# The big scratch tensor of a two-network float32 kernel, laid out in another order in SBUF

## What is computed

```python
def first_block(h):                      # per layer i of 2
    h = h + 0.5 * swiglu(rmsnorm(h, ffn1_norm[i]), gate, up, down)     # 1024 -> 2816 -> 1024
    u = rmsnorm(h, mix_norm[i]) @ w_in[i]
    y = concat([y_mla, y_mlstm, y_fnet])                               # the mixers, from u
    h = h + y @ w_out[i]
    h = h + 0.5 * swiglu(rmsnorm(h, ffn2_norm[i]), gate, up, down)
    e = rmsnorm(p[i] @ ple_w_proj[i], ple_post_norm[i])
    h = h + sigmoid(rmsnorm(h, ple_gate_norm[i]) @ ple_w_gate[i]) * e

def second_block(x):                     # per layer l of 2
    mod = cond @ ada_w[l] + ada_b[l]                                   # shift, scale, gate
    h = rmsnorm_2(x, norm_mix[l]) * (1 + sc_m) + sh_m
    x = x + gt_m * hybrid_mixer(h, ...)      # window attention, HGRN2, gated delta rule, w_out
    h = rmsnorm_2(x, norm_ffn[l]) * (1 + sc_f) + sh_f
    x = x + gt_f * swiglu_2(h, gate, up, down)
```

## Time and profile before

| | us |
|---|---|
| median of three timed executions (lowest, highest) | 3909.55 (3904.68, 3914.15) |
| the profiled execution: its time | 3909.84 |
| its span, first to last instruction | 3908.1 |
| TensorE busy (share of the span) | 3732.5 (96%) |
| VectorE busy | 2213.7 (57%) |
| ScalarE busy | 1296.8 (33%) |
| GpSimd busy | 730.3 (19%) |

### The profile page before, as it was taken

One profiled execution on the slowest core, in us unless ns is written; L12 is line 12 of the kernel. 1 busy time (PEld: TensorE's weight loads), 2 busy tenths in 40 slices (PEclk: granted clock), 3 DMA queues, 4 the chain that ended last, 5 costly groups with the idle time before them and its releaser, 6 DMA issues. The chain is left out here.

```text
span 3908.1 us, 42134 instructions
## 1 busy us (share of the span) xinstructions
PE 3732.5 (96%) x16630; PEld 2876.4 (74%) x16630; DVE 2213.7 (57%) x2994; ACT 1296.8 (33%) x1873; POOL 730.3 (19%) x434
## 2 busy tenths in 40 slices
PE   8999998999999999998999989888999999989999
PEld 6888733888878888635888866686888766867887
DVE  6554557655564455457655576665544557755443
ACT  3222235522242223335422343444222343443221
POOL 3432002343213430001444013020000020200000
PEclk9999998999999999998999999798999998989999
DMA  4443201444323442102444322001233220012232
GB/s 169 140 135 107 94 13 33 134 138 129 121 93 126 134 132 93 60 23 81 138 131 137 97 78 62 4 1 65 87 95 100 81 77 21 1 49 82 95 99 81
DMA packets 92947, 345.43 MB, mean 88 GB/s; under 512 B 10832, under 2 KB 11088, under 8 KB 91856
## 3 DMA queue, kind: packets, MB, share of 16 engines
q1 hardware_dynamic: 92752, 342.74, 27.1%
HBM read 340.60 MB, written 2.10 MB: 88 GB/s over the span
## 5 line engine op out<-in xcount | busy, mean ns | idle before, releaser
L383 ACT ACTIVATE w_hi<-raw 128x1024 fp32r<-128x1024 f32 (+2 forms) x540 | 559.5, 1038 | 1927.9 <-PE ps L327 1912.6
L325 PE MATMUL ps<-xs_hi,w_hi 128*128 128x512 f32 x2472 | 982.1, 397 | 35.6 <-DVE xs_lo L544 16.5
L326 PE MATMUL ps<-xs_lo,w_hi 128*128 128x512 f32 x2472 | 970.5, 393 | 0.0
L327 PE MATMUL ps<-xs_hi,w_lo 128*128 128x512 f32 x2472 | 970.1, 392 | 0.0
L393 DVE TENSOR_TENSOR w_lo<-raw,w_hi 128x1024 fp32r<-128x1024 f32 (+2 forms) x540 | 673.9, 1249 | 125.9 <-ACT w_hi L383 125.7
L325 PEld LDWEIGHTS ps<-xs_hi,w_hi 128*128 128x128 f32 x2472 | 468.8, 190 | 161.1 <-issue 33.7
L326 PEld LDWEIGHTS ps<-xs_lo,w_hi 128*128 128x128 f32 x2472 | 469.9, 190 | 99.0 <-issue 3.6
L327 PEld LDWEIGHTS ps<-xs_hi,w_lo 128*128 128x128 f32 x2472 | 469.2, 190 | 98.9
L325 PE MATMUL ps<-hd_hi,w_hi 128*128 128x512 f32 x1320 | 527.0, 399 | 4.7 <-DVE hd_lo L486 3.5
L327 PE MATMUL ps<-hd_hi,w_lo 128*128 128x512 f32 x1320 | 523.8, 397 | 0.0
L326 PE MATMUL ps<-hd_lo,w_hi 128*128 128x512 f32 x1320 | 523.8, 397 | 0.0
(11 more groups left out here) (454 smaller groups left out, 4341.1 us busy)
## 6 DMA issues: line engine op xcount, KB each, us to landing
raw<-in_ffn_gu SPq DMA_DIRECT2D x264, 512.0 KB, 3.8
arena<-in_ada SPq DMA_DIRECT2D x64, 768.0 KB, 5.6
raw<-in_ffn_dn SPq DMA_DIRECT2D x96, 448.0 KB, 3.4
raw<-in_in_t SPq DMA_DIRECT2D x60, 512.0 KB, 3.7
raw<-in_ffn_dn SPq DMA_DIRECT2D x48, 512.0 KB, 3.5
raw<-in_out SPq DMA_DIRECT2D x32, 512.0 KB, 3.7
raw<-in_pleg SPq DMA_DIRECT2D x16, 512.0 KB, 3.6
raw<-in_in_r SPq DMA_DIRECT2D x8, 512.0 KB, 3.8
```

The costliest lines, as they stand in the source:

```text
L325: T.matmul(bank, lhs_hi(k), rhs_hi(k), start=(first and k == 0), stop=False)
L326: T.matmul(bank, lhs_hi(k), rhs_lo(k), start=False, stop=False)
L327: mm = T.matmul(bank, lhs_lo(k), rhs_hi(k), start=False, stop=(last and k == kt - 1))
L383: A.activation(self.hi[:, n % HL, 0:size], raw[:, n % RAW, 0:size], ACT.Copy).then_inc(self.high_done, 1)
```

## The change

Only numbers change: where the parts of the arena lie. Not one instruction is added, removed or moved on any engine, nor is any wait.

```diff
     SPLIT = 2 * DT * S
-    REST = 13088
-    SPARE = 1808
-    LINE = 128
-    HD_AT, REST_AT = 0, SPLIT
-    X_AT = SPLIT + REST
+    REST = 13064
+    SPARE = 1920
+    LINE = 32
+    HD_AT, X_AT = 0, SPLIT
     HL_AT = X_AT + SPLIT
     SPARE_AT = HL_AT + 2 * HL * CW
-    WORDS = SPARE_AT + SPARE
+    REST_AT = SPARE_AT + SPARE
+    WORDS = REST_AT + REST
     fence_at = -(-nc.sbuf_base // LINE) * LINE
...
     def work_space():

-        return Space(HD_AT + DT * S, SPLIT - DT * S), Space(X_AT, WORDS - X_AT)
+        return Space(HD_AT + DT * S, SPLIT - DT * S), Space(X_AT, REST_AT - X_AT)
```

## The result

The changed kernel takes 3877.19 us (median of four, 3871.53 to 3878.38) against 3909.28 us for the kernel before in the same comparison: a ratio of 0.9917, 95% interval 0.9904 to 0.9929, so 32.1 us less. The profiled execution took 3878.38 us around a span of 3876.6. Forecast were 3879.8 us and a gain of 30.0.

A forecast was written before the change was run, and what follows sets the result against it. TensorE's pace was taken to bound the kernel; 25.2 + 4.3 + 0.5 = 30.0 us off 3909.8 gave 3879.8 us (80%), own range 3872 to 3890, range for all 3870 to 3900.

The forecast's parts named there:

- The bound: Whole kernel: TensorE's own pace sets the time, weight preparation is ahead, and the gain reaches the end undiminished.
- `hd`: 25.2 us: 3960 matmuls streaming hd, put at distance 0, speed up to the pace of xs: 25.2 us gained.
- `ys`: 4.3 us: 768 matmuls streaming ys, put at distance 0, each gain 5.6 ns: 4.3 us.
- The swapped product: 0.5 us: 96 matmuls with hd as weights go from 232.3 to 226.8 ns: 0.5 us gained.
- `xs` and alignment: nothing: xs and w by w keep distance 0 by 512; starts 32 bytes past a multiple of 128 cost nothing.
- the rival of 3960 us: All split matmuls: the shorter pace needs starts at multiples of 64 or 128 bytes, so 50 us slower; 7% chance.
- Regions: 3948 us: Split matmuls: an operand below byte 131072 costs pace; 42.8 us lost on hd and xs, ys gains 4.3; 5% chance.
- Mixers and other engines: 0 with 2 us each way: Mixers' moved buffers and other engines' operations: no change, with 2 us each way allowed for the mixers' small operations.
- A multiple of 512 bytes: Split matmuls: about 226.8 ns where stream and weights lie such a distance apart, 232.3 to 233.3 ns elsewhere.

The follow-up runs named there:

- `old_order`: Kernel before with REST 13120 words in place of 13088, putting xs and the ring 128 bytes further; 3876.63 us against 3909.37, ratio 0.9918.
- `order_alone`: Changed kernel with a 128-byte gap that restores the old remainders by 512 between stream and weights; 3907.18 us against 3906.23 for the kernel before, ratio 1.0004.
- `w_lo_off`: Changed kernel with only w_lo moved, by 128 bytes; 3924.81 us against 3906.23 for the kernel before, ratio 1.0058.
- `all_off`: Changed kernel with the weight ring moved by 128 bytes, so xs, hd and ys are at remainder 384; 3938.36 us against the kernel before's 3906.23.

## Why the prediction was right

*The bound.* It took TensorE's pace as what sets the time, and a shorter pace as fully paid out. TensorE's busy time fell by 30.9 us and the span by 31.5; no wait took the place.

*`hd`: 25.2 us.* The stretches over `hd` are 25.7 us shorter, here and in `old_order`.

*`ys`: 4.3 us.* Its mean interval at full clock went from 232.6 to 227.0 ns, which gives 4.3 us. In the lengths of the stretches the granted clock hid it in the first pair of traces (-0.1 us) and added to it in `old_order` (-5.7), so no single trace shows the term by its stretches.

*The swapped product: 0.5 us.* Measured 0.5.

*`xs` and alignment: nothing.* Right: every split operand now starts 32 bytes past a multiple of 64, and 226.7 ns is the same pace. This also removes the rival of 3960 us. It was the step with the thinnest ground, and that ground was misread, so here the forecast was lucky. The prediction took the 68 matmuls of line 317 as a row in which some read an operand 32 bytes past a multiple of 64 and some don't. By the offsets (`uq` and `ukv` start at words 7688 and 9992 of the mixers' part, the other operand of each product on a multiple of 256 bytes) every one of them reads one such operand, so the row had nothing to compare with. Nor does it hold a fitting distance: the weights are 32 bytes ahead by 256 in 52 of the 68 and 32 behind in the other 16. The comparison with a fit takes the attention's matmuls of the same line, whose operands lie a multiple of 512 bytes apart. In the kernel before:

```profile
537.66 3.60 PE L317 MATMUL ps<-arena 128*128 128x512 f32 x8
```

Without the 0.59 us of the last matmul that is 3.01 / 7 = 430 ns, and the 68 of the earlier trace rows give 28.83 / 67 = 430 ns: plain float32 keeps its pace at a misfit and at a fit.

*Regions: 3948 us.* Refuted by the changed kernel itself, where `hd` and most of `xs` are below byte 131072 with the weights above, and by `order_alone`.

*Mixers and other engines: 0 with 2 us each way.* The operations read again (lines 317, 393, 978 and 1001) have kept their durations to 1 ns. The mixers and the rest still moved by -4.8 us, while the granted clock there rose from 0.876 to 0.881. The allowance of 2 us was too small for a single trace, though the medians absorb it.

*What was wrong.* "A multiple of 512 bytes" was stated where the rows could only say "not 384 and not 128"; the period is 256. It made no difference to this change, since 512 is a multiple of it. And the picture of two reads in each other's way needs a detail that `w_lo_off` showed: both the load ahead of a stream and the load behind it count. The 27 us expected of `w_lo_off` for one misfit tile out of three was too small for that reason; 48 were measured.

The rule that the prediction weighed, two independent read ports for TensorE, which never waits on anyone (the Trainium skill, "SBUF — State Buffer", "Who interferes with whom"), does not give the pace of this loop, if it is read to say that layout costs nothing: eleven kernels with the same instructions ran their split matmuls at 226.7 to 234.3 ns by nothing but an offset. The other rule of that page of the Trainium skill, lines of 16 bytes ("Specifications (TRN2)"), agrees with the trace as far as absolute alignment goes, a shift by 32 bytes of both operands costing nothing, and says nothing of the distance between the two.

What stays open is what the two reads share. The experiments say that equal low eight bits of the byte address avoid the cost, that plain float32 matmuls, which load new weights only every 0.43 us, don't show it, and that it vanishes at 1.2 GHz (0.43 us per matmul with a misfit, and 0.43 us without, at 2661 us above). They don't say what makes one misfit settle in a rhythm of 233.3 ns and another in one of 229.0. Distances under 32 bytes weren't tried.

## What to carry to other kernels

Where TensorE loads new weights for every matmul and is the bound, compare the pace of consecutive starts, not the durations, for each pair of streamed tensor and weight tensor. If products of the same shape differ by a few per cent, look at the remainders by 256 of the two start addresses; making them equal costs a few words of padding and needs no other order. Here one number, `REST`, was worth 0.8% of the kernel.

## What the runs showed of the hardware

- With weights loaded for each matmul of 512 fp32r columns, the pace at 2.4 GHz was 226.7 ns where stream and weights agreed by 256 bytes, and 229.0 to 234.3 ns where they didn't. 32 bytes of difference gave 233.4.
- A single misfit weight tile in a sequence was paid twice, 5.7 ns while it loads and 7.3 ns while it is used; misfits on both sides of an interval cost 6.5 ns together (`w_lo_off`, and the earlier trace rows).
- At 1.2 GHz there was no such cost (426 to 427 ns per matmul with a misfit and without).
- Plain float32 matmuls of 512 columns kept 430 ns at distances of 32 and of 0 by 256 bytes (line 317).
- One and the same misfit can run at two paces: over `hd` at a remainder of 128 by 256, 233.3 ns in one chunk and 232.4 in another, in `all_off` and in the trace before.
- VectorE's operations with two inputs in SBUF, with GpSimd idle, took 692 ns for 512 elements with the inputs 0, 128 or 224 bytes apart by 512 (lines 978 and 1001, both kernels).
